# PEER retrieval: V rows gathered for 64 tokens and two experts at a time, and summed as two 64 wide column tiles

## The reference

```python
g = jax.nn.softmax(best_s, axis=-1)                     # 8 heads x 16 experts per token
def block(args):                                        # 128 tokens
    xt, et, gt = args
    act = jax.nn.gelu(jnp.einsum('td,thkd->thk', xt, u[et]), approximate=False)
    return jnp.einsum('thk,thkd->td', gt * act, v[et])
```

## Time and profile before

| what | us |
|---|---|
| median of 3 runs (3503.16 to 3509.37) | 3503.28 |
| the profiled execution | 3502.22 |
| its span | 3500.1 |
| PE busy | 2942.9 (84%) |
| DVE busy | 2341.0 (67%) |
| POOL busy | 2008.2 (57%) |
| ACT busy | 814.6 (23%) |

### The profile page before, as it was taken

The page is one execution under the profiler, slowest core; times in us unless marked ns, Lnnn a source line. Parts: engine busy times, 40 slices in busy tenths (PEclk is TensorE's granted clock), DMA queues, the critical chain, the costliest instruction groups (busy, mean ns, idle before and its releaser), DMA issues.

```text
span 3500.1 us, 34723 instructions
## 1 busy us (share of the span) xinstructions
PE 2942.9 (84%) x10960; PEld 1660.0 (47%) x10960; DVE 2341.0 (67%) x5884; ACT 814.6 (23%) x1924; POOL 2008.2 (57%) x2085
## 2 busy tenths in 40 slices
PE   7786898888997899888987799888998789976777
PEld 6465355533554355444554445544554445522222
DVE  6229756886578765887477855786648866596554
ACT  3111421133111422133211332114221232211111
POOL 1003765666565664666555655666547655577775
PEclk9897999999999999999999999999999999998999
DMA  7787999999999999999999999999999999999998
GB/s 275 259 299 266 409 409 409 408 409 402 409 402 408 399 405 403 407 409 390 405 409 408 397 351 409 409 408 370 354 409 409 409 346 350 390 404 410 409 409 339
DMA packets 387256, 1346.12 MB, mean 385 GB/s; under 512 B 41793, under 2 KB 44865, under 8 KB 386433
## 3 DMA queue, kind: packets, MB, share of 16 engines
q0 software_dynamic: 294912, 1073.87, 78.0%
q1 hardware_dynamic: 91008, 265.83, 20.1%
q10 hardware_dynamic: 1152, 4.19, 0.3%
HBM read 1334.03 MB, written 35.39 MB: 391 GB/s over the span
## 4 chain that ended last, share of the span: by engine, by line
PE 43%; DMA 25%; DVE 14%; POOL 9%; issue 6%; ACT 3%; SPq 0%; DVEq 0%; ACTq 0%; POOLq 0%
PE ps_sum L1212 19%; DMA rows<-in_peer_u,ids_u 9%; PE ps_p L979 7%; DMA rows<-in_peer_v,ids_v 6%; DMA rows<-in_peer_v,ids_u 5%; POOL rows L802 5%; PE ps_s L1127 5%; POOL rows L792 4%; DVE rows L1986 4%; DMA w_ring<-packed 2%; PE ps_s L1065 2%; PE ps_p L1073 2%; DVE feat_b L1873 1%; PE ps_p L1047 1%; DVE feat_b L1869 1%
## 5 line engine op out<-in xcount | busy, mean ns | idle before, releaser
L1212 PE MATMUL ps_sum<-rows,diag 128*128 128x512 f32 x3584 | 1748.0, 631 | 271.9 <-DMA rows<-in_peer_v,ids_v 129.2
L1986 DVE CUSTOM_DVE_ANT_0 rows<-h_cur,rows 128x1024 f32<-128x1024 f32 x1024 | 1228.1, 1220 | 539.7 <-DMA rows<-in_peer_u,ids_u 527.0
L792 POOL DMA_INDIRECT rows<-in_peer_u,ids_u x1024 | 1005.4, 982 | 720.7 <-issue 498.8
L1212 PEld LDWEIGHTS ps_sum<-rows,diag 128*128 128x128 f32 x3584 | 684.1, 201 | 1166.4 <-issue 1047.8
L802 POOL DMA_INDIRECT rows<-in_peer_v,ids_v x512 | 493.5, 964 | 452.2 <-PE ps_sum L1212 295.6
L802 POOL DMA_INDIRECT rows<-in_peer_v,ids_u x512 | 494.4, 966 | 267.8 <-issue 127.3
L1466 ACT ACTIVATE diag<-ident,acts 128x128 f32<-128x128 f32 x896 | 327.4, 394 | 1057.4 <-PE ps_sum L1212 757.5
L979 PE MATMUL ps_p<-hT,w_ring 128*128 128x128 f32 x2944 | 367.8, 286 | 36.1 <-DMA w_ring<-packed 18.0
L979 PEld LDWEIGHTS ps_p<-hT,w_ring 128*128 128x128 f32 x2944 | 362.0, 202 | 68.6 <-issue 42.3
L1772 DVE CUSTOM_DVE_ANT_0 e<-ps_s,bias_t 128x256 f32<-128x256 f32 (+6 forms) x96 | 74.2, 773 | 177.5 <-PE ps_s L1065 70.6
L2007 DVE SCALAR_TENSOR_TENSOR x_cur<-rows,acts,x_cur 128x1024 f32<-128x1024 f32 x128 | 164.0, 1282 | 13.4 <-DMA rows<-in_peer_v,ids_v 13.4
(11 more groups left out here) (280 smaller groups left out, 2325.7 us busy)
## 6 DMA issues: line engine op xcount, KB each, us to landing
w_ring<-packed SPq DMA_DIRECT2D x343, 512.0 KB, 7.7
w_ring<-in_wstream SPq DMA_DIRECT2D x65, 512.0 KB, 5.3
packed<-in_wstream SPq DMA_DIRECT2D x49, 512.0 KB, 7.9
rows<-in_peer_u,ids_u POOLq DMA_INDIRECT x1024, 13.3
rows<-in_peer_v,ids_u POOLq DMA_INDIRECT x512, 10.7
rows<-in_peer_v,ids_v POOLq DMA_INDIRECT x512, 15.4
bias_rows<-rows SPq DMA_DIRECT2D x5, 1024.0 KB, 12.8
bias_t<-in_x SPq DMA_DIRECT2D x8, 512.0 KB, 6.2
```

Source lines behind the costliest of these rows:

```text
L792: pool.indirect_dma_start(u_rows[:, j % G_RING, :], None, peer_u, bass.IndirectOffsetOnAxis(ap=ids_u[:, j:j + 1], axis=0)).then_inc(u_land ...
L1212: ins = pe.matmul(ps_sum[:, c * 512:(c + 1) * 512], diag[:, n % 4, :], v_rows[:, j % G_RING, c * 512:(c + 1) * 512], start=(n == 0), stop= ...
L1986: dve.tensor_tensor_reduce(row, h_cur[:, :], row, 1.0, 0.0, ALU.mult, ALU.add, dots[:, p:p + 1]).then_inc(u_used, 1)
```

## The change

The v rows are gathered in another arrangement. Column 2i of the new `ids_v` holds, for the tokens 0 to 63, expert 2i in partitions 0 to 63 and expert 2i + 1 in partitions 64 to 127; column 2i + 1 holds the same two experts for the tokens 64 to 127. A gather still brings 128 rows of 4 KB. `g_cur` and `acts` are kept in the same arrangement: `by_group` yields the four quarters, and each copy or gelu becomes four instructions on 64 partitions and half the columns. A diagonal is now two 64x64 identities above each other (`ident_pair`) scaled by `coef`: 128x64, for every row, in a ring of 8. Its product with a gathered slot sums both experts into 64 rows of `ps_sum`: rows 0 to 63 for an even slot (`low`), 64 to 127 for an odd one (`high`). PE takes two slots at a time, alternating low and high for each half of D. `on_vector`, line 2007 and `v_added` go. u rows and dot products stay as they are.

```diff
-SHARE = 8
-SUM_ROWS = EXPERTS - EXPERTS // SHARE
-SUM_SLOTS = G_RING - G_RING // SHARE
+GROUP = P // 2
+DIAGS = 8
...
-        diag = sb("diag", [P, 4, P])
+        diag = sb("diag", [P, DIAGS, GROUP])
+        ident_pair = sb("ident_pair", [P, GROUP])
...
+        low, high = slice(0, GROUP), slice(GROUP, P)
+
+        def by_group(first, last):
+
+            for at, own in ((low, low), (low, high), (high, low), (high, high)):
+                column = slice(first + (own is high), last, 2)
+                row = slice(first + (at is high), last, 2)
+                yield at, column, own, row
...
             def gather_v(j):
 
-                if on_vector(j):
-                    wait_next(v_added)
-                else:
-                    wait_next(v_used)
-                ids = ids_u if j < FIRST else ids_v
+                wait_next(v_used)
                 pool.indirect_dma_start(v_rows[:, j % G_RING, :], None, peer_v,
-                                        bass.IndirectOffsetOnAxis(ap=ids[:, j:j + 1], axis=0)).then_inc(v_landed[j % G_RING], 16)
+                                        bass.IndirectOffsetOnAxis(ap=ids_v[:, j:j + 1], axis=0)).then_inc(v_landed[j % G_RING], 16)
...
-            def add_row(bp, p):
-                bp, j = row_of(bp, p, SUM_LAG)
-                if j is not None and not on_vector(j):
-                    n = sum_index(j)
-                    pe.wait_ge(diag_made, bp * SUM_ROWS + n + 1)
+            def add_rows(bp, p):
+                bp, last = row_of(bp, p, SUM_LAG)
+                if last is None or last % 2 == 0:
+                    return
+                pair = (last - 1, last)
+                pe.wait_ge(diag_made, bp * EXPERTS + last + 1)
+                for j in pair:
                     pe.wait_ge(v_landed[j % G_RING], bp * (16 * EXPERTS // G_RING) + 16 * (j // G_RING + 1))
...
-                    for c in range(2):
-                        ins = pe.matmul(ps_sum[:, c * 512:(c + 1) * 512], diag[:, n % 4, :], v_rows[:, j % G_RING, c * 512:(c + 1) * 512],
-                                        start=(n == 0), stop=(n == SUM_ROWS - 1), skip_group_check=True)
-                    ins.then_inc(v_used, 1)
+                for c in range(2):
+                    for j, own in zip(pair, (low, high)):
+                        ins = pe.matmul(ps_sum[own, c * 512:(c + 1) * 512], diag[:, j % DIAGS, :], v_rows[:, j % G_RING, c * 512:(c + 1) * 512],
+                                        start=(last == 1), stop=(last == EXPERTS - 1), skip_group_check=True)
+                        if c:
+                            ins.then_inc(v_used, 1)
...
+            def pair_ident():
+
+                act.wait_ge(consts_made, 3)
+                for half in (low, high):
+                    copy(ident_pair[half, :], ident[half, half]).then_inc(pair_made, 1)
+                act.wait_ge(pair_made, 2)
...
-                    act.activation(acts[:, s * STEP:(s + 1) * STEP], dots[:, s * STEP:(s + 1) * STEP], ACT.Gelu).then_inc(acts_made, 1)
+                    for at, column, own, row in by_group(s * STEP, (s + 1) * STEP):
+                        ins = act.activation(acts[at, column], dots[own, row], ACT.Gelu)
+                    ins.then_inc(acts_made, 1)
...
-                if j is not None and not on_vector(j):
-                    n = sum_index(j)
+                if j is not None:
...
-                    act.wait_ge(v_used, bp * SUM_ROWS + (n + SUM_SLOTS - 3))
-                    act.activation(diag[:, n % 4, :], ident[:, :], ACT.Copy, scale=coef[:, j:j + 1]).then_inc(diag_made, 1)
+                    act.wait_ge(v_used, bp * EXPERTS + (j + G_RING - DIAGS + 1))
+                    act.activation(diag[:, j % DIAGS, :], ident_pair[:, :], ACT.Copy, scale=coef[:, j:j + 1]).then_inc(diag_made, 1)
...
             def hand_first_ids(b):
...
+                for at, column, own, row in by_group(0, FIRST):
+                    dve.tensor_copy(ids_v[at, column], ids_next[own, row])
                 dve.tensor_copy(ids_u[:, 0:FIRST], ids_next[:, 0:FIRST]).then_inc(ids_handed, 1)
...
-                dve.tensor_copy(g_cur[:, :], g_next[:, :]).then_inc(g_handed, 1)
+                for at, column, own, row in by_group(0, EXPERTS):
+                    ins = dve.tensor_copy(g_cur[at, column], g_next[own, row])
+                ins.then_inc(g_handed, 1)
...
-                dve.tensor_copy(ids_v[:, FIRST:], ids_u[:, FIRST:]).then_inc(v_ids_handed, 1)
+                for at, column, own, row in by_group(FIRST, EXPERTS):
+                    ins = dve.tensor_copy(ids_v[at, column], ids_u[own, row])
+                ins.then_inc(v_ids_handed, 1)
...
-                at, j = row_of(bp, p, SUM_LAG)
-                if j is not None and on_vector(j):
-
-                    dve.wait_ge(v_landed[j % G_RING], at * (16 * EXPERTS // G_RING) + 16 * (j // G_RING + 1))
-
-                    dve.wait_ge(v_added, at * (EXPERTS // SHARE) + (j + G_RING) // SHARE)
-                    dve.wait_ge(coef_made, at * STEPS + (j // STEP + 1))
-                    dve.scalar_tensor_tensor(x_cur[:, :], v_rows[:, j % G_RING, :], coef[:, j:j + 1], x_cur[:, :], ALU.mult, ALU.add)\
-                       .then_inc(v_added, 1)
```

31 lines of the change are left out of this document (13 added, 18 removed).

## The result

The change made the kernel slower: 3560.34 us, median of 4 runs (3555.38 to 3574.28), beside 3504.2 us for the kernel before in the same comparison. The ratio is 1.0166, 95% interval 1.0144 to 1.0187. I had predicted 3432 us with a range of 3415 to 3490 us. Both the direction and the range were wrong.

The account below looks back on a forecast made before the run. DMA, capped at 409.6 GB/s, was taken to bound the kernel. Span 3500.1 - 71 (dips) - 2 (end) + 1.4 (first copies) = 3428.5 us, giving a time of 3432 us, range 3415 to 3490.

Parts of the forecast that it names:

- The cap and the loss under it: DMA between 350 and 3,450 us: capped at 409.6 GB/s, 84 us lost below it, 61 in late attention dips.
- The cost of a row: Sums on PE: 0.86 us a row with tiles side by side, within bounds of 0.86 and 1.72 us.
- the 60% of 1748: Sign in the changed profile: busy time of ps_sum falls to some 60% of 1748 us.
- The part freed in the dips: Stretch 2830 to 2950: sums fall from 52.4 to 29.9 us, giving PE 22.5 back against 26.0 us of lost DMA time.
- the term of 71 us: Gain in the late attention dips from shorter PE sums: 85% of 84 us lost under the cap, 71 us off.
- Rival 3: Attention dips come from chain latency, not PE's load, and stay: 3496 to 3510 us; chance 0.05.
- Rival 1: PE tiles overlap only in part, or the clock falls: costs 15 to 60 of 71 us, 3447 to 3492; chance 0.16.
- Slots: v slots on POOL's queue: a first row waits up to 2.56 us for the second; costs nothing unless PE is late.
- Rival 2: PE's two column tiles run one after the other: slower, near 3580 us, 3540 to 3640; chance 0.13.
- The change of the tiling mode: PE array drains at up to 128 mode changes a block: at 0.33 us each, 42 us a loop, near 3465 us.
- The estimate for two tiles: PE sums: 1.6 times for two column tiles, 1.08 us a row, giving 3460 us.
- ACT, DVE, the small copies: ACT and DVE work counted as hidden; only block 0's first copies cost, 0 to 2.7 us, taken as 1.4 us on.

Follow-up runs that it names:

- f0: The changed kernel itself, unaltered, run again as a control beside the kernel before: 3560.33 us, ratio 1.0163.
- e1: The kernel before with its sums over columns 512 to 1023 only, one row at a time, 128 wide: 3490.0 us, ratio 0.9963.
- g2: The changed kernel with both rows of a pair summed into the same lower 64 partitions, so they can't run side by side: ratio 1.0569.
- f1: The changed kernel with each row summed at its own position, with its own waits and its slot given back at once: 3529.48 us, ratio 1.0063.

## Why the prediction was wrong

- **The cap and the loss under it: right.** The rate between the stretches is 402 to 409 GB/s before and after, and the time lost in the stretches explains the 72 us of span. Before, they lost 52 of the 84 us that I had counted.
- **The cost of a row: right for a pair by itself, too low in the mix.** I chose 0.86 us a row; a pair takes 1.94 us, 0.97 a row with its loads, and 3.41 at the lower clock (I had said 3.4). The sums' 1252.8 us are more than the 60% of 1748 that I named, 72%. By my own 0.86 us, 1024 rows would be 881 us. Pairs at the lower clock are the main reason that the rows show.
- **The part freed in the dips: too large, and wrong in effect.** This is the step that failed: "with the factor they take 29.9, so PE gets 22.5 us back", and from it 85% of 84 us. I set TensorE's freed time equal to time of the dip. Already the factor was off: with 0.57 the 280 us of sums in the stretches would have become 160, 120 us less. They became 214, a factor of 0.76 (207 and 0.74 in f0). That 66 lies near my 71 is chance, for the 71 are us of dip and not of sums. And what was freed did not shorten the dips: the front's matmuls took 79 us more and TensorE idled 43 us more. Halving alone (e1) gave 14 us, none of it in the stretches. So the term of 71 us should have been 14 for halving alone, with nothing for the stretches, and what the pairs cost was missing from the sum.
- **What I overlooked in the rows.** I read "PE is busy 90 to 94%" as a load that binds. It was two things at once: a chain of short steps between TensorE, DVE and ACT, and sums that filled its gaps. With half of the sums gone, e1 shows TensorE idle for 125 us in the stretches, where 75 were idle before, and the length hardly changed (566 against 555 us). Part of the gaps was hidden under the sums; the rest of what was freed, 44 us, went into slower matmuls of the front. Rival 3 (3496 to 3510) had dips that stay in place with PE idle in them, and 0.05 of the chances; for e1 it is nearly the truth.
- **The clock: seen and priced too low.** Rival 1 says that a TensorE which works less will be at the lower level more often, and then "only bursts of attention work pay". It priced that at 15 to 60 of 71 us, a part of the gain and never more. In the stretches the clock went from 0.95 to 0.76 (0.79 in f0), and the same matmuls took 79 us more where 66 were won (67 and 73 in f0), up to 22 of them by the estimate for 64 wide groups and not by the clock. The waits in the last stretch fit the reading that slower matmuls lengthen a chain in which TensorE is a link; no run shows its size.
- **"Slots": wrong.** I wrote that the pair's wait costs nothing unless PE is late. In the dips PE is late, and that is where it counts. Row by row is 31 us faster than pairs; some 8 of them are the slot's later release, with intervals that just overlap. The other 23 are clock and lump together, which the runs don't tell apart.
- **Rival 2: right by 20 us in its time (3580), for a reason that didn't occur.** Its column tiles in series never happened.
- **The change of the tiling mode: half of what I feared, and there.** In rival 1 I cited the Trainium skill, "TensorEngine Tiling (Array Packing)", Key Properties, that a change of the tiling mode drains the array. I put 0.33 us on each of 128 changes a block, 42 us a loop. The trace agrees that there is a cost, and has it at about 0.35 us for a 64 wide group with the change before and the one after it. With 64 pairs a block that is an estimate of up to 22 us of TensorE a loop. Whether it is a drain or weights that can't be loaded ahead, the rows don't say.
- **The estimate for two tiles: too low.** The 1.6 times for two column tiles that I estimated from the Trainium skill, "TensorE: Matmul & The Clock Gate", Measured speedup vs the span model, is exceeded here: a pair takes 1.94 us on two tiles and 3.65 us on one (g2), 1.9 times.
- **ACT, DVE, the small copies: nothing seen against them.** Dropping three of the four gelus showed no gain. The 164 us of DVE's products that went bought nothing either; DVE's wait for u rows rose from 527.0 to 651.8 us.
- **What stays open.** Row by row, with every slot released in time and a clock of 0.936, is still 26 us slower than before. It has all rows on TensorE where one in eight was DVE's, coefficients for two groups of tokens, and the front at 234 us in place of 200. By the same estimate (0.29 us each) its 108 or so 64 wide groups in the stretches account for up to 31 of these 34 us; the clock there is 0.90 where it was 0.95, so it has a share too. No run takes away one of these alone. The kernel before with all rows on TensorE wasn't tried, nor 64 wide sums with fewer changes between widths.

The cause as far as shown: less work in the sums doesn't shorten the attention stretches (e1), and doing them in pairs costs 31 us against the same sums row by row (f1). That the lower clock, and in a smaller part the change between widths, take back what the sums gave is argued from durations. No run changes either alone, and the last 26 us are open.

## What to carry to other kernels

An engine that is 90% busy in a dip need not be the cause of it. Ask what is left of the stretch when its filler work is taken away: if the rest is a chain of short steps over several engines, halving the filler uncovers the chain's gaps. A test as cheap as leaving out half of the work (e1: 14 us for half of the sums) tells what such a change can bring before it is written.

Less work on TensorE can slow its remaining work down, so cost the neighbours' matmuls at both clock levels and not the changed ones alone. And in a kernel that lives on slots and gathers, do each row as soon as it is there: joining rows into pairs cost more here than the pairs saved, and rows that stood together in TensorE's order overlapped on the two tiles without being joined (f1).
